# Tile 0's norm taken out of the way of its queries, a ones column in the mLSTM's values, the half switch and the dense loads moved ahead

## The reference, cut to what matters

```python
for layer in range(2):
    hn = rmsnorm(h, norm_mix_g[layer])
    h += attn_mlstm_mixer(hn, ...) if layer == 0 else multiscale_pool_mixer(hn, ...)
    h += peer_ffn(rmsnorm(h, norm_ffn_g[layer]), wq, keys, u, v)   # per layer
return rmsnorm(h, norm_f)

def rmsnorm(x, g):   return x * rsqrt(mean(x * x) + EPS) * g

# mLSTM, per head, direction and 128-token chunk
C_loc = einsum('l,ld,le->de', w, k, v);  n_loc = einsum('l,ld->d', w, k)
num   = inter_w * (q @ C_prev) + Sqk @ v
den   = inter_w * (q @ n_prev) + sum(Sqk)
out   = num / max(|den|, exp(-m))

def peer_ffn(xn, wq, keys, u, v):                # 8 heads, 128 x 128 keys, top 16
    q = (xn @ wq).reshape(tokens, 8, 2, 128)
    s_top, i_top = top_k(q . keys, 16)           # for each of the two key sets
    best, pos = top_k(s_top[0][:, None] + s_top[1][None, :], 16)
    gate = softmax(best)                         # 128 experts per token
    act = gelu(u[expert] . xn)
    return sum((gate * act) * v[expert])
```

## Time and profile before

| | before |
|---|---|
| median of 3 runs | 3032.93 us (3029.3 to 3036.68) |
| the profiled execution's own time | 3032.51 us |
| its span | 3030.7 us |
| PE busy | 2334.3 us (77%) |
| DVE busy | 2126.4 us (70%) |
| POOL busy | 1098.8 us (36%) |
| ACT busy | 822.2 us (27%) |
| DMA moved | 1058.78 MB, 349 GB/s over the span |

### The profile page before, as it was taken

The page is one execution under the profiler, slowest core; times in us unless marked ns, Lnnn a source line. Parts: engine busy times, 40 slices in busy tenths (PEclk is TensorE's granted clock), DMA queues, the critical chain, the costliest instruction groups (busy, mean ns, idle before and its releaser), DMA issues.

```text
span 3030.7 us, 26494 instructions
## 1 busy us (share of the span) xinstructions
PE 2334.3 (77%) x9238; PEld 1710.7 (56%) x9238; DVE 2126.4 (70%) x3103; ACT 822.2 (27%) x2097; POOL 1098.8 (36%) x1028
## 2 busy tenths in 40 slices
PE   8999999788873333699999987888534329999987
PEld 4686555577862322466655556788433216666554
DVE  1242122799999989856666648999997997566666
ACT  1242120112227977100000021122299741000000
POOL 0000000433333333444477614333342435445764
PEclk8999999899985555899999988999755559999998
DMA  5323224899999999899999949999999998999998
GB/s 213 139 111 139 111 111 192 358 421 421 409 373 420 421 375 421 302 410 409 409 409 409 409 196 423 417 420 412 386 421 386 411 421 300 410 409 409 409 409 341
DMA packets 196883, 1058.78 MB, mean 349 GB/s; under 512 B 23952, under 2 KB 24592, under 8 KB 123664
## 3 DMA queue, kind: packets, MB, share of 16 engines
q0 software_dynamic: 147456, 805.37, 65.6%
q1 hardware_dynamic: 49296, 251.74, 21.0%
HBM read 1054.53 MB, written 2.10 MB: 349 GB/s over the span
## 4 chain that ended last, share of the span: by engine, by line
DMA 35%; PE 25%; DVE 25%; ACT 10%; issue 3%; POOL 3%; DVEq 0%; SPq 0%; ACTq 0%; POOLq 0%
DMA xnT<-pvg,idx_all 19%; DVE arena L1277 13%; PE bank L1452 6%; DMA arena<-pu,ints 6%; DMA arena<-pvg,idx_all 5%; ACT arena L818 4%; DMA arena<-pu,idx_all 4%; PE bank L1537 3%; ACT arena L827 2%; DVE h L1317 2%; PE bank L1692 2%; ACT arena L823 2%; PE low L1800 2%; PE bank L1779 1%; PE low L1657 1%
## 5 line engine op out<-in xcount | busy, mean ns | idle before, releaser
L1277 DVE CUSTOM_DVE_ANT_0 arena<-arena,low 128x2048 f32<-128x2048 f32 x424 | 955.3, 2284 | 96.8 <-PE low L1765 36.9
L1800 PE MATMUL low<-arena 128*128 128x512 f32 x2048 | 907.8, 602 | 40.3 <-DMA arena<-pvd 39.4
L1800 PEld LDWEIGHTS low<-arena 128*128 128x128 f32 x2048 | 599.3, 296 | 348.6 <-DMA arena<-pvd 91.4
L522 POOL DMA_INDIRECT arena<-pu,idx_all x200 | 218.1, 1090 | 974.0 <-DVE idx_all L1246 596.3
L1317 DVE SCALAR_TENSOR_TENSOR h<-arena,cst,h 128x1024 f32<-128x1024 f32 x248 | 318.1, 1286 | 165.7 <-DMA arena<-pvg,idx_all 164.7
L1317 DVE SCALAR_TENSOR_TENSOR h<-xnT,cst,h 128x1024 f32<-128x1024 f32 x248 | 317.4, 1285 | 159.3 <-DMA xnT<-pvg,idx_all 158.4
L1779 PE MATMUL bank<-arena 128*128 128x128 f32 x768 | 195.4, 434 | 297.7 <-ACT arena L827 297.7
L538 POOL DMA_INDIRECT arena<-pvg,idx_all x256 | 291.8, 1140 | 231.0 <-DVE h L1317 164.1
L538 POOL DMA_INDIRECT xnT<-pvg,idx_all x256 | 292.8, 1144 | 221.0 <-DVE h L1317 157.9
L1779 PEld LDWEIGHTS bank<-arena 128*128 128x128 f32 x768 | 167.9, 322 | 325.9 <-ACT arena L827 324.9
L564 ACT ACTIVATE h<-low 128x512 f32<-128x512 f32 x8 | 4.3, 589 | 953.8 <-PE low L1800 953.8
(11 more groups left out here) (253 smaller groups left out, 2163.5 us busy)
## 6 DMA issues: line engine op xcount, KB each, us to landing
arena<-pvd SPq DMA_DIRECT2D x256, 512.0 KB, 6.8
arena<-w_proj SPq DMA_DIRECT2D x22, 2048.0 KB, 7.6
arena<-wq SPq DMA_DIRECT2D x16, 2048.0 KB, 12.1
arena<-w_out SPq DMA_DIRECT2D x9, 2048.0 KB, 8.5
gB<-gains SPq DMA_DIRECT2D x4, 1024.0 KB, 10.2
arena<-pu,ints POOLq DMA_INDIRECT x256, 12.3
xnT<-pvg,idx_all POOLq DMA_INDIRECT x256, 13.7
arena<-pvg,idx_all POOLq DMA_INDIRECT x256, 13.7
```

What stands on the lines that cost most here:

```text
L522: nc.gpsimd.indirect_dma_start(U[t][slot], None, pu[L], bass.IndirectOffsetOnAxis(idx_p[:, d:d + 1] if t else row(n), 0)).then_inc(u_got[t ...
L1277: vec.tensor_tensor_reduce(out=u, in0=u, in1=low[:, :] if staged else xns[0], scale=1.0, scalar=0.0, op0=ALU.mult, op1=ALU.add, accum_out= ...
L1800: ins = mm(psum[2 * t + c][:, 0:VH], W[t][:, :, n], vdense[:, n % DR, c * VH:(c + 1) * VH], start=False, stop=n == NK - 1)
```

## The change

Five parts.

- **Ones column.** `raw` gets a column more for each mLSTM head (`raw_v`, set to 1 once). The two matmuls against V (128x256) and against ones (128x1) become one of 128x257, for `C_loc` and for `Sqk @ v`.
- **Tile 0 without 1/rms.** DVE multiplies tile 0's `h` by the gain in four pieces, each right behind the piece's residual add (`times_gain`), in place of one scaling by 1/rms and gain. PE transposes piece by piece into banks 4, 5, 7, 5 and starts the first query matmuls half way (`first_queries`). The factor 1/rms goes into the softmax's `Exp` and into `Gelu` as ACT's scale. The work that stood between norm and transposes is placed behind the first scores.
- **Half switch.** `duplicate(L, 0)` waits for three dots fewer (those three read the tokens from SBUF), `duplicate(L, 1)` is placed three quads earlier among the spreads.
- **PE's rows.** `on_pe` takes `n % 4 == 0` instead of `n % 4 == 2`.
- **Dense loads.** `pace` reaches NV - 10 instead of NV - 3.

```diff
 def turn_bank(o, t, q):
-    return 0 if o and t else 4
+    if o and t == 0:
+        return (4, 5, 7, 5)[q]
+    return q if o else 4 + q
 def on_pe(n):
-    return PK <= n < HK and n % 4 == 2
+    return PK <= n < HK and n % 4 == 0
 def pace(n):
-    return (NV - 3) * (n - 2) // NK - (NK - n) // 4
+    return (NV - 10) * (n - 2) // NK - (NK - n) // 4
...
 # ACT
-    activation(ex[:, t0:t1], bd[:, t0:t1], ACT.Exp)
+    ins = activation(ex[:, 0], bd[:, 0], ACT.Exp, scale=rs[:, 0:1])
+    if t1 == 2:
+        ins = activation(ex[:, 1], bd[:, 1], ACT.Exp)
-    activation(wv[:, 0], act[:, 0], ACT.Gelu)
+    activation(wv[:, 0], act[:, 0], ACT.Gelu, scale=rs[:, 0:1])
-    norm(1 + 2 * L, 0)
     evac_xt(1 + L, 0)
+    norm(1 + 2 * L, 0)
...
 # DVE
+def times_gain(o, n):
+    cols = slice(n * BANK, (n + 1) * BANK)
+    vec.tensor_tensor(xn0[:, cols], h[:, 0, cols], gB[:, cols], ALU.mult
+                      ).then_inc(s["xn_ready" if n == 3 else "xg_ready"], 1)
 # add_mixer(0) and add_pooled(0), behind each piece's add
+    v.wait_ge(s["h_ready"], i + 1)
+    times_gain(1, n)
-    norm(1 + 2 * L, 0)
     evac_xt(1 + L, 0)
+    mean_square(1 + 2 * L, 0)
+    v.wait_ge(s["root_done"], TB * (1 + 2 * L) + 1)
+    link(vec.reciprocal(rs[:, 0:1], rt[:, 0:1]))
 # dot
-    staged = t or hk >= PK
+    staged = t or PK <= hk < HK - 3
...
 # PE, mLSTM
-    mm(psum[2 + c][:, 0:MD], kwc, raw[:, d, R_MV + hd * MD:R_MV + (hd + 1) * MD], start=True, stop=True)
-    mm(psum[2 + c][:, MD:MD + 1], kwc, ones[:, 0:1], start=True, stop=True)
+    mm(psum[2 + c][:, 0:MD + 1], kwc, raw_v[:, d, hd], start=True, stop=True)
 # PE, duplicate
-    pe.wait_ge(s["dot_done"], L * NDOT + ND0 + hf * HP)
+    pe.wait_ge(s["dot_done"], L * NDOT + ND0 + hf * HP - (0 if hf else 3))
 # PE, head
-    else:
-        project_mlstm(1, 3)
-    transpose_xn(1 + L, 1 + 2 * L, 0, xn0)
+    transpose_xn(1 + L, 1 + 2 * L, 0, xn0, range(3))
-    queries(L, 0, 0, 0, 0, 1)
+    first_queries(L, range(0, KC // 2))
+    transpose_xn(1 + L, 1 + 2 * L, 0, xn0, range(3, 4))
+    first_queries(L, range(KC // 2, KC))
     scores(L, 0, 0, 0, 1)
     if L == 0:
-        project_mlstm(1, 2)
+        project_mlstm(1, 3)
...
-    if q == QUADS - 4:
+    if q == QUADS - 7:
         duplicate(L, 1)
```

More of the change, by code:

```diff
@@ L580, in norm @@
                     e.wait_ge(s["pool_mm"], KC // 2)
+                if o in (1, 3) and t == 0:
+                    dst = square0
                 if o in (0, 1, 3):
@@ L596, in evac_raw @@
                     e.wait_ge(s["raw_done"], TB * r + t + 1)
-                    activation(raw[:, t, r * BANK:(r + 1) * BANK], psum[4 + t][:, :], ACT.Copy
-                               ).then_inc(s["raw_evac"], 1)
+                    if N_QKV <= r < N_QKV + N_MV:
+                        two = BANK // MD
+                        dst = raw_v[:, t, two * (r - N_QKV):two * (r - N_QKV + 1), 0:MD]
+                        src = psum[4 + t][:, :].rearrange("p (m c) -> p m c", m=two)
+                    else:
+                        at_ = r * BANK if r < N_QKV else R_MO + (r - N_QKV - N_MV) * BANK
+                        dst, src = raw[:, t, at_:at_ + BANK], psum[4 + t][:, :]
+                    activation(dst, src, ACT.Copy).then_inc(s["raw_evac"], 1)
             e.wait_ge(s["one_set"], 1)
@@ L864, in _ @@
                 stage_xn(L, 0)
+                if L == 0:
+                    route_exp(L, 1, 0, 1)
                 for hd in range(2):
@@ L1593, in mlstm @@
                         kwc = kw[:, d, hd, c * P:(c + 1) * P]
[L1594 to L1595 removed]
+                        mm(psum[2 + c][:, 0:MD + 1], kwc, raw_v[:, d, hd], start=True, stop=True).then_inc(s["c_mm"], 1)
                 if i:
@@ L1694, in queries, with first_queries @@
                 ins.then_inc(s["q_mm"], 1)
+            def first_queries(L, ks):
+                if ks[0] == 0:
+                    pe.wait_ge(ld_wq[0], 16 * (4 * L + 1))
+                    if L:
+                        pe.wait_ge(s["q_ready"], EVENTS * L)
+                for k in ks:
+                    if k % 8 == 0:
+                        pe.wait_ge(s["xt_act"], 4 * (1 + L) + k // 8 + 1)
+                    elif k % 8 == 4:
+                        pe.wait_ge(s["xt_dve"], 4 * (1 + L) + k // 8 + 1)
+                    for p_ in range(2):
+                        ins = mm(psum[6][:, p_ * S:p_ * S + P], wq_slots[0][:, k, p_ * P:(p_ + 1) * P],
+                                 xnT[:, k, 0:P], start=k == 0 and p_ == 0, stop=k == KC - 1 and p_ == 1)
+                if ks[-1] == KC - 1:
+                    ins.then_inc(s["q_mm"], 1)
             def scores(L, hd, ev_, t0, t1):
```

67 lines of the change are left out of this document (41 added, 26 removed).

## The result

The changed kernel takes 3007.49 us (median of 4 runs, 3006.05 to 3009.70) against 3034.44 (3029.30 to 3036.68): ratio 0.992, 95% interval 0.9903 to 0.9937 (the two medians divide to 0.9911, inside the interval). It is faster, but by 25 to 27 us instead of 38. The profiled execution took 3007.43 us, its span is 3005.6 us against 3030.7: 25.1 us of difference to explain.

A forecast was written before the change was run, and what follows sets the result against it. PE bounds the kernel before 545 us, then DMA bytes plus moments when the DMA engines have nothing to do. Terms 4.5 + 2 + 13.0 + 0 + 4 + 3.2 + 11.3 = 38.0 us give 2994.5 us; 2983 to 3008 holds 8 in 10.

The forecast's parts named there:

- PE's rows two sooner: u stage: same rows and gathers, PE gets them sooner but POOL's stream meets PE's gathers sooner too; taken as 0.
- the rival: "Slower": POOL's in-order waits for PE grow by 4.4 us each, 123 us in all, holding up gathers; chance 0.04.
- Half switch and first duplicate: Both layers: DVE resumes 6.5 us sooner at the second duplicate, 6.4 and 6.6 us; first duplicate 0, bounds 0 and 4.2.
- It can only move up by these 2.08: First duplicate: starts 2.08 us after PE's last `dot_u`, so it can't move by three dots (6.6); counted 0.
- Ones column: mLSTM stage, PE-bound: 32 matmuls of 128x1 at 0.14 us each saved, 4.5 us, bounds 2 and 6.
- Heads: Starts of both layers: queries begin sooner, 2 us in layer 0 (bounds 1 and 9), 11.3 in layer 1 (8 and 12).
- the gate at the fifth gather: Layer 0's head: the fifth gather waits for all of tile 1's projections, so it opens only 1.6 to 2.1 us sooner.
- the pause: Layer 1's head: PE's pause of 6.62 us before the transposes goes, as PE runs straight on from the pooling projection.
- the slow matmuls behind it: Layer 1's head: queries took 9.34 us behind PE's pause, 7.38 in layer 0; without a pause 7.4 was taken.
- Dense loads: Ends of both layers: dense sums end sooner, 4 us in layer 0 (bounds 0 and 9), 3.2 in layer 1 (-2 and 6).
- the gather tail eats the lead: Dense loads' lead takes DMA time from gathers; both tails give nothing, 38.0 - 7.2, 3001.5 us; chance 0.20.

The follow-up runs named there:

- a_rows2: The changed kernel with PE's rows back at n % 4 == 2: 2998.38 us, ratio 0.988.
- b_rows0: The kernel before with PE's rows at n % 4 == 0 and nothing else: 3044.85 us, ratio 1.0041.
- a_pick1: The changed kernel with DVE's picks two rows sooner (behind row 1 of a block instead of row 3): 3001.29 us, ratio 0.9893.
- b_dups: The kernel before with both duplicates changed and nothing else: 3024.76 us, ratio 0.9976.
- a_pair: The changed kernel with PE's rows at 2 and the pairs of matmuls (128x256 and 128x1) instead of 128x257: 3007.28 us, ratio 0.9916.
- h_only: The changed kernel with every part but the heads undone: 3015.85 us, ratio 0.9949 to the kernel before.
- a_pace3: The changed kernel with pace back at NV - 3: 3013.55 us, ratio 0.9931.
- b_half: The kernel before with the second duplicate three quads sooner and nothing else: 3022.65 us, ratio 0.9963.
- b_r1p2: The kernel before with PE's rows at 1 instead of 2 and picks behind row 2 instead of row 3: 3034.53 us, ratio 1.0007.
- the best version: The changed kernel with PE's rows at 1 and the picks behind row 2: 2989.53 us, ratio 0.9859; once more, 2988.86 us.
- b_dup0: The kernel before with the first duplicate let go three dots sooner and nothing else: 3024.27 us, ratio 0.997.

## Why the prediction was right or wrong

The direction held, and so did the mechanisms, but for PE's rows and the first duplicate; the size was off by 11 to 13 us. Term by term, forecast and measured:

- **PE's rows two sooner: 0 forecast, 9 to 11 us lost.** This is the step that failed ("I take 0"), by a_rows2 (9.1 or 10.7 us) and b_rows0 (10.2). I argued that the longest wait was 6.4 us and the DMA share 1.01 through all of them, so that growth was covered. The waits were: even in windows of 8 us the share stays between 0.96 and 1.04 from 601 to 849 us. But cover is what is issued ahead, here 7 to 8 us behind the last issue; waits of 10.7 us outlast it. And I moved PE's rows and left the pick where it was: the first row of each group of four now comes two dots earlier to the same pick, PE waits 15.6 us for it at the longest instead of 9.8, and its 14 us of queries follow behind that. I had the rival, with the place and its price per wait, and gave it 0.04 because I read a covered wait as a wait with room to grow. POOL's waits for PE grew by 49.9 and 42.5 us, three quarters of the rival's 123, and 9 to 11 us came of it: most was covered even so. That the cost goes through these waits is argued from single windows; a_pick1 took them away and DVE waited as long for gathers as with them.
- **Half switch and first duplicate: 13.0 + 0 forecast, 7.4 to 9.9 measured.** At the switches 6.0 and 7.1 us came, as forecast; the rest of these kernels gave some of it back, in b_dups 6.7 us ahead of layer 1's switch. The first duplicate's 0 holds only next to the other; alone it gives the same again. What I said ("It can only move up by these 2.08") looked at its start, and neither at how long it then takes nor at what PE does behind it.
- **Ones column: 4.5 forecast, 6.4 measured in its stage** (5.1 by spans and 8.9 by medians, a_pair). The mechanism is right, the price was too low and the bound of 6 with it: the earlier trace rows has the first of two pairs, which costs 0.14 us more than its 128x256 matmul, and the second costs 0.22. By the Trainium skill ("TensorE: Matmul & The Clock Gate", section "Wait — 56ns, not 53.3ns?") it would have been an estimated 1.6 us. That is a floor, and the two entries of a 128x1 matmul do start 0.03 us apart in the trace; the next matmul only follows 0.11 us later, so the floor is no price.
- **Heads: 2 + 11.3 forecast, 15.4 measured** (h_only), 0.7 and 11.0 by the table. Of all steps this one was read best: the gate at the fifth gather, the pause, the slow matmuls behind it.
- **Dense loads: 7.2 forecast, 4.5 to 6 measured.** Layer 1's end gave 3.4 of 3.2; layer 0 gave 1.4 of 4. The rival "the gather tail eats the lead" (whose 3001.5 should read 3001.7) is half true: from first to 201st add takes 395.6 us instead of 392.8 in layer 0, and only the last 47 are 4.1 us shorter. With `pace` back (a_pace3) the former is 393.0 again. The Trainium skill ("DMA: Bandwidth & Descriptors", section "SWDGE vs HWDGE vs iDMA") says that the queues take turns at a DMA engine; by this rule loads let go sooner slow the gathers, and the trace agrees, with 2.8 us.

Added up from these numbers, the parts give 22 to 31 us; measured were 25 to 27. The sum is loose, since each part was measured in another kernel and the parts overlap. With the rows at 2 the gain is 36.2 us against 38.0, and that is in part luck: the ones column and the heads gave about 2 us each more than forecast, the duplicates 3 to 6 and the dense loads 1 to 3 less.

What stays open: layer 1's stretch from first gather to 164th dot takes 523.8 to 525.4 us in the kernel before, h_only, b_half and b_r1p2, and 525.6 to 530.8 in every other kernel with rows at 1 or 2, without one part that all the long ones share and the short ones lack. Some of it is scatter, for the two profiles of the best version have 527.5 and 525.6. The rest isn't settled. Nor is why rows at 1 do best, nor how the rows' cost divides between POOL's waits for PE and the place of DVE's routing.

## What to carry to other kernels

A wait that costs nothing because enough is queued is a threshold, not slack: before lengthening it, count the time that the transfers in flight last, and set the new wait against that. An average share over 250 us can't tell how near the edge a wait is: the 4 us at 0.10 would take 0.014 off it. Where consumers in several engines are placed by hand relative to each other (rows, picks, bursts), move them together, or try the neighbours: three places for the rows and three for the picks spread over 20 us here (3009.05 to 2988.86). Two edits that shorten the same chain are worth one of them, so a sum over parts needs the question what is last when the first has been done.

## What the runs showed of the hardware

A 257th column costs nothing that can be read: matmuls of 128x257 and of 128x256 in float32 both start 0.43 us apart. A separate 128x1 matmul costs 0.14 us behind the first 128x256 and 0.22 behind the second, and slows the next entry by up to 0.08 us more. So 32 of them were worth 6.4 us, in all twenty profiles.

The same four matmuls of 128x512 (`duplicate`) take 5.37 us behind a pause of PE of 2.08 us, with a granted clock of 0.68 (before, layer 0), and 3.60 us without the pause, with a granted clock of 1.00 (b_dup0).
